# Bonus sums and rotations on GpSimd beside the RWKV rounds, one table for tanh and sigmoid, forget gate logits in the rounded format

## The reference, cut to what matters

```python
# first block, RWKV-7 part (16 heads of 64)
p = p + (prev - p) * mu
r, k, v, xw, xa, xg = split_cols(p, RWKV_SPLITS)
w = -softplus(-(w0 + tanh(xw) @ w_decay_up)) - 0.5
a = sigmoid(a0 + xa @ a_up)
g = sigmoid(xg) @ g_up
kk = heads(k * k_k); kk = kk / max(sqrt(sum(kk * kk)), 1e-12)
k = k * (1.0 + (a - 1.0) * k_a)
_, y = scan(step, s0, (r4, w4, k4, v4, kk, a4))          # the recurrence
yn = (y - mean) * rsqrt(var + 64e-5) * lnx_w + lnx_b      # mean, var per head
bonus = sum(r4 * k4 * r_k, axis=-1, keepdims=True) * v4
rwkv = (yn + bonus) * g
# first block, attention part: partial rotary rotation of q, k and index queries and keys, then top-64 selection
# second block: forget gate of the second attention
log_f = log_sigmoid(flogit + b_forget)                    # flogit: 8 columns of h @ w_in_2
```

## Time and profile before

| | us |
|---|---|
| median of 3 runs | 3494.64 (3486.57 to 3496.1) |
| the profiled execution, its own time | 3493.31 |
| its span, first to last instruction | 3491.6 |
| mean granted TensorE clock | 0.871 of full speed |
| busy: PE, DVE, ACT, POOL | 2531.9, 1686.1, 1091.1, 2582.2 |

### The profile page before, as it was taken

The page is one execution under the profiler, slowest core; times in us unless marked ns, Lnnn a source line. Parts: engine busy times, 40 slices in busy tenths (PEclk is TensorE's granted clock), DMA queues, the critical chain, the costliest instruction groups (busy, mean ns, idle before and its releaser), DMA issues.

```text
span 3491.6 us, 42762 instructions
## 1 busy us (share of the span) xinstructions
PE 2531.9 (73%) x15849; PEld 1985.6 (57%) x15849; DVE 1686.1 (48%) x2277; ACT 1091.1 (31%) x2113; POOL 2582.2 (74%) x1835
## 2 busy tenths in 40 slices
PE   7996778899999999989999899306701750472067
PEld 5884577678998899879898678302300320131023
DVE  4003366424220132231321435897698879788954
ACT  5442423455444444454445655100000000000000
POOL 7897802868999999988675577886687578657852
PEclk9997899999999999999999999758955975786589
DMA  5666400345665666546454354899999999999998
GB/s 177 182 190 161 139 3 3 104 144 163 184 188 189 181 182 191 186 153 175 129 150 121 109 177 151 316 427 427 427 427 427 427 427 427 427 426 427 427 427 346
DMA packets 239894, 868.01 MB, mean 249 GB/s; under 512 B 18594, under 2 KB 20772, under 8 KB 173028
## 3 DMA queue, kind: packets, MB, share of 16 engines
q0 software_dynamic: 73776, 536.97, 36.5%
q1 hardware_dynamic: 163414, 316.11, 29.8%
q10 hardware_dynamic: 2540, 12.75, 1.3%
HBM read 860.24 MB, written 2.10 MB: 247 GB/s over the span
## 4 chain that ended last, share of the span: by engine, by line
PE 50%; POOL 23%; DMA 11%; DVE 7%; issue 6%; ACT 2%; DVEq 0%; POOLq 0%; SPq 0%; ACTq 0%
PE acc L1867 20%; PE acc L1877 19%; DMA zone<-in_peer_v,zone 11%; POOL zone L713 9%; POOL lasting L713 9%; POOL w_lo L597 5%; PE acc L1873 3%; PE acc L1996 3%; PE acc L2422 2%; DVE lasting L1808 1%; PE acc L2311 1%; DVE zone L1417 1%; PE acc L2242 0%; PE acc L1914 0%; DMA lasting<-in_w_mix_out 0%
## 5 line engine op out<-in xcount | busy, mean ns | idle before, releaser
L597 POOL TENSOR_TENSOR w_lo<-lasting,w_hi 128x512 fp32r<-128x512 f32 (+1 forms) x1184 | 1591.6, 1363 | 332.1 <-ACT w_hi L758 307.0
L758 ACT ACTIVATE w_hi<-lasting 128x512 fp32r<-128x512 f32 (+1 forms) x1184 | 742.8, 632 | 925.3 <-PE acc L1867 458.6
L2422 PE MATMUL acc<-zone,lasting 128*128 128x512 f32 x512 | 257.7, 662 | 699.9 <-ACT lasting L1235 639.1
L2422 PEld LDWEIGHTS acc<-zone,lasting 128*128 128x128 f32 x512 | 105.7, 212 | 851.3 <-ACT lasting L1235 498.4
L713 POOL DMA_INDIRECT zone<-in_peer_v,zone x128 | 189.1, 1477 | 177.7 <-DVE lasting L1808 74.7
L1877 PE MATMUL acc<-x_hi,w_hi 128*128 128x256 f32 (+1 forms) x1856 | 305.9, 287 | 16.8 <-DVE x_lo L1546 6.0
L1778 DVE CUSTOM_DVE_ANT_0 zone<-lasting,zone 128x2048 f32<-128x2048 f32 x128 | 293.4, 2292 | 30.4 <-DMA lasting<-in_peer_u,zone 20.3
L1778 DVE CUSTOM_DVE_ANT_0 zone<-zone 128x2048 f32<-128x2048 f32 x128 | 293.4, 2292 | 22.9 <-DMA zone<-in_peer_u,zone 13.6
L1877 PE MATMUL acc<-x_lo,w_hi 128*128 128x256 f32 (+1 forms) x1856 | 299.4, 283 | 0.0
L1877 PE MATMUL acc<-x_hi,w_lo 128*128 128x256 f32 (+1 forms) x1856 | 299.1, 283 | 0.0
L713 POOL DMA_INDIRECT zone<-in_peer_u,zone x128 | 256.2, 2002 | 50.1 <-issue 37.5
(11 more groups left out here) (417 smaller groups left out, 3890.7 us busy)
## 6 DMA issues: line engine op xcount, KB each, us to landing
lasting<-in_w_in SPq DMA_DIRECT2D x200, 512.0 KB, 3.6
lasting<-in_w_up SPq DMA_DIRECT2D x128, 512.0 KB, 3.8
lasting<-in_w_down SPq DMA_DIRECT2D x128, 512.0 KB, 4.3
lasting<-in_w_mix_out SPq DMA_DIRECT2D x32, 512.0 KB, 3.7
lasting<-in_w_out SPq DMA_DIRECT2D x32, 512.0 KB, 3.6
lasting<-in_peer_w_query SPq DMA_DIRECT2D x32, 512.0 KB, 3.6
lasting<-in_w_kv_cross SPq DMA_DIRECT2D x16, 512.0 KB, 3.8
lasting<-in_w_q_cross SPq DMA_DIRECT2D x8, 512.0 KB, 3.6
```

Of the source, the lines that this page charges most:

```text
L597: pool.tensor_tensor(w_lo[:, k, 0:width], ring[:, slot, s % SLOT_SLABS, 0:width], w_hi[:, k, 0:width].bitcast(FP32), ALU.subtract).then_in ...
L758: act.activation(w_hi[:, s % PARTS, 0:width], ring[:, slot, s % SLOT_SLABS, 0:width], ACT.Copy).then_inc(hi_ready, 1)
L2422: last = pe.matmul(bank(4 * t + c), diag[:, n // 2, k], rows_buf[2 * n + k][:, c * CHUNK:(c + 1) * CHUNK], start=hx % 2 == 0 and i == 0 an ...
```

## The change

- The bonus sums leave DVE's elementwise part. POOL makes them from the scaled r and k (whose exponentials cancel) once `s_el` says that a tile is finished, with `bonus_row` and `kk_sq`.
- POOL's rotations now wait for `s_el` of both tiles, so that they, then the bonus sums, run beside the rounds of the recurrence.
- Mean and variance of y for `t` = 0 are taken by POOL as soon as the second round is done, those of `t` = 1 after the fourth; they use a buffer of their own, `early_sq`.
- ACT loads the table set `sigmoid_and_others` ahead of tanh and sigmoid.
- The logits: POOL waits for the DMA of `w_logit`, rounds it and takes the remainder (two instructions on 128 by 128 elements) before the first `w_lo` of `fox_kv`; PE makes 48 matmuls in the rounded format (three products of 16 slabs) instead of 32 in fp32.
- Six spare scratch places of the rounds are given up, so that the new buffers have room.

```diff
-        spots += [zs + i * n4 for i in range(26 - len(spots))]
+        spots += [zs + i * n4 for i in range(20 - len(spots))]
...
-                    sp.dma_start(params[:, 3], A["r_k"][0].rearrange("h n -> (h n)").partition_broadcast(P)).then_inc(s_par, 16)
+                    sp.dma_start(bonus_row, A["r_k"][0].rearrange("h n -> (h n)").partition_broadcast(P)).then_inc(s_par, 16)
...
             for k in range(4):
                 pool.wait_ge(acc_free[k], G["mix"].used0[k] + 1)
+            pool.wait_ge(s_el, TILES)
             for t in range(TILES):
...
-            for u in range(2):
-                g_wait(pool, len(PAIRS) - 1, "y", u, 1)
+            for t in range(TILES):
+                pool.wait_ge(s_el, t + 1)
+                step(TT(kk_sq, p[:, t, 0:R_W], p[:, t, R_W:2 * R_W], ALU.mult))
+                step(TT(kk_sq, kk_sq, bonus_row, ALU.mult))
+                step(head_sums(bonus[:, t], heads(kk_sq), kk_sq))
+
             pool.wait_ge(s_lnx, 32)
...
             for t in range(TILES):
+                for u in range(2):
+                    g_wait(pool, 2 * t + 1, "y", u, 1)
                 y = key_t[:, t]
-                step(head_sums(yst[:, 0, t], heads(y), y_sq))
+                step(head_sums(yst[:, 0, t], heads(y), early_sq))
...
             pool.memset(ones, 1.0).then_inc(s_c2, 1)
+            pool.wait_ge(s_meta, 16)
+            step(pool.tensor_copy(logit_w[0], w_logit))
+            TT(logit_w[1], w_logit, logit_w[0].bitcast(FP32), ALU.subtract).then_inc(s_lw, 1)
             rests("fox_kv", "fox_q", "sb_k", "sb_q", "sb_v", "fox_gate", "out2_fox", "out2_sb")
...
+            act.preload_act_table_set("sigmoid_and_others")
             act.wait_ge(s_mixed, TILES)
...
                 step(STT(k_, tmp, 1.0, k_, ALU.add, ALU.mult))
-                step(TT(tmp, r_, k_, ALU.mult))
-                step(TT(tmp, tmp, params[:, 3], ALU.mult))
-                step(RED(bonus[:, t], heads(tmp), AX, ALU.add))
                 dve.wait_ge(s_ksd, t + 1)
...
-                pe.wait_ge(s_meta, 16)
+                pe.wait_ge(s_lw, 1)
                 pe.wait_ge(s_c2, 1)
                 pe.wait_ge(s_vr, 2)
-                for n in range(2):
+                for n, (wp, xp) in enumerate(((logit_w[0], xT[0]), (logit_w[0], xT[1]), (logit_w[1], xT[0]))):
                     for s_ in range(SLABS):
-                        last = pe.matmul(bank(6)[0:HEADS2, 0:CTX], w_logit[:, s_], xT[n][:, s_].bitcast(FP32),
-                                         start=n == 0 and s_ == 0, stop=n == 1 and s_ == SLABS - 1)
+                        last = pe.matmul(bank(6)[0:HEADS2, 0:CTX], wp[:, s_], xp[:, s_],
+                                         start=n == 0 and s_ == 0, stop=n == 2 and s_ == SLABS - 1)
```

More of the change, by code:

```diff
@@ L132, in build @@
             pass
+        LOGIT_AT = BASE + 26688
         parts, place = {}, 0
@@ L136, in build @@
                              ("hid_hi", BASE, FF * SEQ // 2 // P), ("hid_lo", BASE + FF * SEQ // 2 // P, FF * SEQ // 2 // P),
-                             ("mem_hi", MEM_AT, TILES * D), ("mem_lo", MEM_AT + TILES * D, TILES * D), ("", TOTAL, 0)):
+                             ("mem_hi", MEM_AT, TILES * D), ("mem_lo", MEM_AT + TILES * D, TILES * D),
+                             ("logit_hi", LOGIT_AT, SLABS * HEADS2), ("logit_lo", LOGIT_AT + SLABS * HEADS2, SLABS * HEADS2), ("", TOTAL, 0)):
             if off > place:
@@ L234, in build @@
         params = at(z, 4, R_W); z += 4 * R_W
-        kk_sq = at(z, R_W)
+        kk_sq = at(z, R_W); z += R_W
+        bonus_row, early_sq = at(z, R_W), at(z + R_W, R_W)
         w0 = gate[:, 1]
@@ L246, in build @@
         spots = [X0 + i * n4 for i in range(7)] + [x_rest + 3 * R_W + i * n4 for i in range(3)]
-        spots += [zs + i * n4 for i in range(26 - len(spots))]
+        spots += [zs + i * n4 for i in range(20 - len(spots))]
+        assert max(spots) + n4 <= zs + 5 * R_W
         scr = [at(spot, n4) for spot in spots]
@@ L313, in build @@
         cumf = at(z, TILES, HEADS2); z += TILES * HEADS2
+        logit_w = tuple(part_at(LOGIT_AT + n * SLABS * HEADS2, SLABS, HEADS2) for n in range(2))
         assert z <= TOTAL, z
@@ L519, in build @@
             "cum_ready", "cum_turned", "cum_column"))
+        s_lw = sem("logit_weights_split")
         s_fs, s_fp, s_fr, s_fn, s_l, s_fg, s_mg, s_erow = (sem(n) for n in (
@@ L677, in _ @@
             for t in range(TILES):
+                for u in range(2):
+                    g_wait(pool, 2 * t + 1, "y", u, 1)
                 y = key_t[:, t]
-                step(head_sums(yst[:, 0, t], heads(y), y_sq))
+                step(head_sums(yst[:, 0, t], heads(y), early_sq))
                 step(pool.tensor_scalar(yst[:, 0, t], yst[:, 0, t], 1.0 / R_HEAD, None, ALU.mult))
                 step(TT(heads(y), heads(y), bc(yst[:, 0, t]), ALU.subtract))
-                step(TT(y_sq, y, y, ALU.mult))
-                step(head_sums(yst[:, 1, t], heads(y_sq), y_sq))
+                step(TT(early_sq, y, y, ALU.mult))
+                step(head_sums(yst[:, 1, t], heads(early_sq), early_sq))
                 pool.tensor_scalar(yst[:, 1, t], yst[:, 1, t], 1.0 / R_HEAD, 64e-5, ALU.mult, ALU.add).then_inc(s_yv, 1)
+                pool.wait_ge(s_yv, t + 1)
             pool.wait_ge(s_ysd, 1)
```

## The result

The changed kernel takes 3471.61 us (median of 5 runs, 3468.72 to 3477.78) against 3494.24 for the kernel before in the same call (5 runs): a ratio of 0.9945, 95% interval 0.9929 to 0.9962. The two medians are 22.6 us apart; the ratio is that of the means, and by it the gain is 19.2 us (13 to 25). The forecast was 3475.5 with a range of 3468 to 3485. The profiled execution took 3470.53 us with a span of 3468.7, against 3493.31 and 3491.6 before, so 22.9 us of span have to be accounted for; the sum of the prediction had 17.8.

The account below looks back on a forecast made before the run. No engine was full in the elementwise part; PE was busy 118.7 of 132 us in the rounds and throughout the logits. Gains of 1.4+3.2+2.4+0.6-1.5+1.5+8.7+1.5 = 17.8 us from 3493.31 gave 3475.5 us, range 3468 to 3485.

Parts of the forecast that it names:

- Table: ACT ahead of the low-rank products: one table set for tanh and sigmoid removes the second load; gain 1.4 us, bounds 0 and 1.45.
- Bonus off DVE: Elementwise part: without the bonus sums DVE goes on once ACT's root is there; gains 3.2 and 2.4 us for the two tiles.
- Rotations: Elementwise part: with POOL's rotations gone, the first tile's DVE steps behind the root are no longer lengthened; gain 0.6 us.
- Rounds: Rounds of the recurrence: POOL's moved work holds some DVE steps with both inputs in SBUF; loss 1.5 us, bounds 0 and 25.
- Rival A: Rounds: long POOL steps hold all 12 two-input DVE steps, loss 25 us, time 3499; chance 0.03 (half held, 3486.6: 0.08).
- Index: Index part behind the rounds: only the second tile's y sums remain on POOL, so DVE's L1417 is not held; gain 1.5 us.
- Logits: Logits on PE: 48 matmuls in the rounded format at 0.1254 us each, 6.02 us against 14.76; gain 8.7 us.
- Rival B: Logits: matmuls with the narrow stationary operand take 0.23 us each, gain 3.7 instead of 8.7 us, time 3480.5; chance 0.12.
- D: Rival, behind the logits: a third of their 8.7 us gain is lost to waits on ACT or DVE, time 3478.4; chance 0.08.
- Norm: `mix2` norm ahead of `fox_kv`: POOL's wait and short steps let about two of DVE's four L1538 through quickly; gain 1.5 us.
- Rival C: ACT's tanh and sigmoid: the table set does not serve both and a load remains between them, time 3476.9; chance 0.04.

## Why the prediction came out as it did

It held in direction and range. The forecast was 3.9 us too high; by its own steps, against the profiled execution (the misses partly cancel: the elementwise part gained 0.9 less than forecast, the rounds lost 1.5 less, the norm gained 2.2 more):

- **Table, 1.4.** 1.38 measured at the copy, and no drain beyond the load: its removal gives 1.37 and not 2.66 (the figure by the Trainium skill, ScalarE: Activation LUTs, "What ACT_TABLE_LOAD costs"). The step that failed is the next one, what is late then. I looked at the landing of the weights, not at ACT's root, which DVE needs and which stands in ACT's list behind a gate copy of 1.03 us and a table load of 1.28, and so behind a PE product of 1.12 to 2.08 us, by execution. Net 0.17 between the two executions with and without the edit, 1.07 to 1.48 once the root goes first.
- **Bonus off DVE, 3.2 and 2.4.** Measured 4.12 - 1.63 = 2.5 and 3.77 - 1.80 = 2.0. The mechanism held, both terms were too large: I put the root at its time of before, though it hangs on PE's gate product, which took 1.94 and 2.07 us here for 1.50 and 1.74 before. As this length varies between executions of the same code, part of the miss is chance.
- **Rotations, 0.6.** The elementwise part gained 5.31; less the 4.5 of the bonus that leaves 0.8, near 0.6. What I missed is that the same wait also keeps the bonus off the second tile's steps, which is worth 3.45. It couldn't be seen as a term in the trace of before, since POOL had no bonus there.
- **Rounds, -1.5.** Measured 0.0 in sum: -0.56 in the third round, one step held, as the y sums' late variant shows, and 0.54 gained in the first two, which no step of mine has. Over the kernels whose POOL isn't filled the four rounds took 129.6 to 131.6 us, so the 0.0 is partly luck. My timetable had POOL's short adds beside L1400; they were over. Rival A was real in mechanism (22.5 us with the bonus six times) and absent in place. One slip in its working: with 9 of 12 steps held the sum gives 3492.9, still faster than before; it is slower from 10.
- **Index, 1.5.** 1.82, undone and restored with the y sums.
- **Logits, 8.7.** 8.80. Rival B fell (0.124 us each with 8 stationary columns). D fell for the norms behind the logits: the products after the norm take 106.7 us in both kernels, and the first 218 us behind the logits are the same to 0.1 us. Further back it is neither shown nor excluded. 1801.4 against 1802.0 us follow the logits here, but over all executions it is 1799.1 to 1807.6 (mean 1804.2) in the ten with the new logits and 1797.0 to 1803.9 (mean 1800.5) in the four with the old. Most of the spread lies in one stretch some 420 us behind the logits, 264 to 273 us long, with a DMA share of 0.78 to 0.81. That behind the logits nothing is tied to a fixed time, as I wrote, was not read from any row.
- **Norm, 1.5.** 3.72, outside my bounds of -1 to 2.5. The mechanism held (the order of POOL and DVE), the size didn't: all four scalings went free, as the weights landed at 5.1 and not 4.0 us, worth 2.2 us at PE's start, and PE then ran its first slabs at a granted clock of 1.00 (2.4 GHz) where before it had 0.50 (1.2 GHz), worth some 1.5 more. That second part can't be counted on. PE had idled 3.04 us ahead of its first product before, and 0.90 after; but with the rotations early it idled 0.87 us, started just as soon, and ran these products at 0.50 all the same: the norm took 20.18 us there and not 18.72. The windows before, after, and with the rotations early:

```profile
1561.00:1563.00 2.00, 2.00 (x11) 2.00 (x11) 0.60 (x3) 0.41 (x1) 0.00 (x0) 0.50 0.00 0
```

```profile
1547.00:1549.00 2.00, 1.38 (x11) 1.39 (x12) 1.48 (x7) 2.00 (x10) 2.00 (x2) 1.00 0.60 147
```

```profile
1550.00:1552.00 2.00, 1.97 (x8) 1.97 (x9) 1.51 (x6) 2.00 (x7) 1.49 (x2) 0.50 0.91 244
```

- **Rival C** fell: no load stands between tanh and sigmoid.
- **What no step covers:** 2.5 us ahead of the change. Over all kernels the table load starts at 391.3 to 396.5 us, in code that is the same, so this is no part of the gain. Without it the span's gain is 20.4 against 17.8.

## What to carry to other kernels

When a step leaves an engine's critical list, price the next wait at what it hangs on, through the list of the other engine: here DVE waited for a root that stood behind a copy it didn't need, and part of what two edits had gained went there; swapping two independent instructions brought back 3 us. Long steps moved to GpSimd cost nothing here only where VectorE read PSUM or waited; filling the place several times over shows what it would cost elsewhere. When one engine's step varies between executions of the same code, look at it in all of them before calling it the effect of an edit. And where two engines reach for the same memory within a microsecond of each other, the trace of before doesn't tell who will be first after a change; take both orders into the range.

## What the runs showed of the hardware that was not expected

- The order in which two engines started, within two microseconds, decided threefold durations: the same four scalings of 128x512 took 1.67 to 1.96 us, 3.95 or 5.50 to 5.73, by POOL's first `w_lo` 1.6 to 2.0 us behind DVE, 0.8 behind or 0.05 to 0.3 ahead.
- The granted clock of an unchanged stretch (650 to 850 us) was 0.96 or 0.97 in twelve of the profiled executions and 0.94 in two, and the products up to the norm took 894.7 to 897.5 us in the twelve, 899.6 and 899.8 in the two. Behind the logits a stretch with a DMA share of 0.8 took 264 to 273 us, in the same code. One execution's span doesn't resolve an edit of 3 us; its stages do.
- The first gate product, the same instruction at the same place, took 1.12 to 2.08 us at a granted clock of 1.00 down to 0.50, by execution. In the kernel before and the four with the same code up to there it was 1.50, 1.67, 1.73, 1.79 and 2.07.
- A short idle time ahead of a product doesn't make sure of its clock: with 0.86 to 0.96 us of idle time the first products of `fox_kv` ran at 1.00 in eight executions and at 0.50 in one.
- The same 64 KB transfer, issued at the same place in the same list, landed after 3.9 to 4.2 us or after 4.8 to 5.1, by kernel. Its cause is open.
